# Differential attention: two maps taken one behind the other on VectorE, head squares on ScalarE

## The reference

```python
def probs(q, k):
    s = einsum(q, k) * scale + bias
    return softmax(where(visible, s, NEG_INF))

w = probs(q1, k1) - lam * probs(q2, k2)        # two maps of one head
out = einsum('bhqk,bkhd->bqhd', w, v)          # 4 heads of 128 columns
# per head: RMS norm over its 128 columns (diff_subln), scaled by 1 - lam_init
```

## Time and profile before

| | |
|---|---|
| median of three runs | 1819.9 us |
| profiled execution | 1820.2 us, its span 1818.9 us |
| TensorE busy | 1634.9 us (90%) |
| VectorE busy | 1139.2 us (63%) |
| ScalarE busy | 767.5 us (42%) |
| GpSimd busy | 53.1 us (3%) |
| read from memory | 217.31 MB |

### The profile page before, as it was taken

How to read it: one execution, slowest core, us unless ns; L and a number is a source line. 1 busy time by engine, 2 the same in 40 slices (tenths; PEclk the granted TensorE clock), 3 DMA queues, 4 the chain that set the end, 5 groups by cost and what they waited for, 6 DMA issues and landing times.

```text
span 1818.9 us, 24216 instructions
## 1 busy us (share of the span) xinstructions
PE 1634.9 (90%) x10180; PEld 1435.5 (79%) x10180; DVE 1139.2 (63%) x1898; ACT 767.5 (42%) x1260; POOL 53.1 (3%) x50
## 2 busy tenths in 40 slices
PE   7988997999989899979999998987799888999887
PEld 6978886999889888869998987766789767785455
DVE  5577556555546665465556668454977757777765
ACT  4545434444434454344444463422312234645334
POOL 0000011000000000100000001000000000000000
PEclk9999999999989899889999999966877799899998
DMA  8543334555545433245556532000002065331041
GB/s 268 164 140 124 109 105 162 178 189 186 186 136 170 132 122 114 95 139 185 185 186 192 183 110 77 1 1 1 1 1 94 0 209 156 114 129 45 23 156 70
DMA packets 151181, 219.94 MB, mean 121 GB/s; under 512 B 6230, under 2 KB 110686, under 8 KB 150432
## 3 DMA queue, kind: packets, MB, share of 16 engines
q1 hardware_dynamic: 151072, 218.39, 37.6%
HBM read 217.31 MB, written 1.06 MB: 120 GB/s over the span
## 4 chain that ended last, share of the span: by engine, by line
PE 72%; DVE 17%; ACT 7%; DMA 3%; issue 1%; SPq 0%; DVEq 0%
PE bank L381 17%; PE bank L383 16%; PE bank L382 16%; DVE weights_low L357 4%; PE bank L1901 4%; PE bank L846 2%; PE bank L1992 2%; PE bank L3227 2%; ACT weights_high L344 2%; PE bank L2187 2%; DVE place L2381 1%; PE bank L459 1%; PE bank L1958 1%; DMA place<-ple_w_dram 1%; PE bank L3188 1%
## 5 line engine op out<-in xcount | busy, mean ns | idle before, releaser
L357 DVE TENSOR_TENSOR weights_low<-place,weights_high 128x1024 fp32r<-128x1024 f32 (+2 forms) x387 | 450.1, 1206 | 189.4 <-ACT weights_high L344 188.9
L344 ACT ACTIVATE weights_high<-place 128x1024 fp32r<-128x1024 f32 (+2 forms) x387 | 378.7, 1031 | 140.7 <-DMA place<-w_down_dram 42.9
L381 PE MATMUL bank<-hT_high,weights_high 128*128 128x256 f32 x1152 | 336.7, 292 | 6.6 <-DVE hT_low L478 5.0
L383 PE MATMUL bank<-hT_high,weights_low 128*128 128x256 f32 x1152 | 329.2, 286 | 0.0
L382 PE MATMUL bank<-hT_low,weights_high 128*128 128x256 f32 x1152 | 328.7, 285 | 0.0
L381 PEld LDWEIGHTS bank<-hT_high,weights_high 128*128 128x128 f32 x1152 | 222.1, 193 | 12.7 <-DVE hT_low L478 5.8
L382 PEld LDWEIGHTS bank<-hT_low,weights_high 128*128 128x128 f32 x1152 | 221.9, 193 | 0.6
L383 PEld LDWEIGHTS bank<-hT_high,weights_low 128*128 128x128 f32 x1152 | 221.3, 192 | 0.0
L1901 PE MATMUL bank<-place,place 128*128 128x128 f32 x624 | 90.8, 312 | 26.2 <-DVE place L2348 10.4
L1901 PEld LDWEIGHTS bank<-place,place 128*128 128x128 f32 x624 | 87.0, 224 | 33.4 <-issue 22.6
L381 PE MATMUL bank<-weights_high,branchT_high 128*128 128x512 f32 x256 | 101.0, 395 | 0.0
(11 more groups left out here) (416 smaller groups left out, 3377.1 us busy)
## 6 DMA issues: line engine op xcount, KB each, us to landing
place<-w_in_dram SPq DMA_DIRECT2D x48, 1024.0 KB, 5.3
place<-w_up_dram SPq DMA_DIRECT2D x32, 1024.0 KB, 5.5
place<-w_down_dram SPq DMA_DIRECT2D x32, 1024.0 KB, 5.0
place<-even_w_in_dram SPq DMA_DIRECT2D x17, 1024.0 KB, 5.3
place<-w_out_dram SPq DMA_DIRECT2D x16, 1024.0 KB, 5.1
place<-odd_w_in_dram SPq DMA_DIRECT2D x16, 1024.0 KB, 5.3
place<-w_branch_dram SPq DMA_DIRECT2D x12, 1024.0 KB, 5.0
place<-ple_gate_dram SPq DMA_DIRECT2D x8, 1024.0 KB, 5.9
```

The lines of the kernel that those rows point to most:

```text
L344: nc.scalar.activation(high[:, lo:hi], self.raw[p % SLOTS][:, lo:hi], ACT.Copy).then_inc(*A("high", p, j))
L357: nc.vector.tensor_tensor(low[:, lo:hi], self.raw[p % SLOTS][:, lo:hi], high[:, lo:hi].bitcast(FP32), ALU.subtract).then_inc(*V())
L381: nc.tensor.matmul(out, left[0], right[0], start=first, stop=False)
L383: return nc.tensor.matmul(out, left[1], right[0], start=False, stop=last)
```

## The change

On VectorE the two maps of a differential head are taken one behind the other, both scores and maxima, and their reciprocals come later together, in a function of their own (`over_sums`). No filling stands between them: the steps are taken in bundles (`steps(count)`), for heads 1 to 3 between the second map's maxima and the reciprocals, and before the head's output is copied. On ScalarE the steps between the exponentials go away for the first eight maps but one bundle behind map 1; the rest of them come behind the copy of the turned probabilities. The counts are set so that from the fifth job on each engine is at the same step at the same place as before. The square and the sum of the heads leave VectorE; ScalarE squares each head with a sum (`squares`, two operations for the two token tiles), heads 0 to 2 behind the next copy of turned probabilities, head 3 behind its own output copy, just ahead of the square root. TensorE's order in attention is the same as before.

```diff
--- before.py
+++ after.py
@@ -1153,9 +1153,15 @@
         V.wait_ge(V)
         nc.vector.tensor_reduce(st[:, 0:1], s[:, 0:S], AX.X, ALU.max, negate=True).then_inc(*V())
         nc.vector.tensor_reduce(st[:, 1:2], s[:, S:], AX.X, ALU.max, negate=True).then_inc(*V("negmax", l, n))
+
+    def over_sums(n):
+        st = f.score_stats(n)
         V.wait_ge(("exp", l, n))
         nc.vector.reciprocal(st[:, 4:6], st[:, 2:4]).then_inc(*V("over_sums", l, n))
-        next(fill, None)
+
+    def steps(count):
+        for _ in range(count):
+            next(fill, None)
 
     def combined(h):
         (n1, n2) = maps_of(h)
@@ -1173,7 +1179,7 @@
         g, h = JOBS[job]
         n, width = maps_of(job)[0], (P, P, VDIM)[g]
         out, sums = f.heads_out[:, :, h * width:(h + 1) * width], f.score_stats(n)[:, 4:6]
-        next(fill, None)
+        steps(1 if job else 2)
         if h == 0 and g:
             V.wait_ge(("headsT", l, g - 1, 3))
         V.wait_ge(("out", l, job), V)
@@ -1185,19 +1191,15 @@
                 ins = nc.vector.tensor_scalar(out[:, t, :], b[:, at_:at_ + width], sums[:, r:r + 1], None, ALU.mult)
             ins.then_inc(*V())
         V.same("free", "out", l, job)
-        next(fill, None)
+        V.same("out_copied", l, job)
+        steps(1)
         if h == BRANCH_HEADS[g] - 1:
             finish_branch(g)
 
     def finish_branch(g):
         if g == 0:
-            sq = f.flat_junk[:, 0:TT * WB]
             ho = f.heads_out.rearrange("p t c -> p (t c)")
-            V.wait_ge(V)
-            nc.vector.tensor_tensor(sq, ho, ho, ALU.mult).then_inc(*V())
-            V.wait_ge(V)
-            nc.vector.tensor_reduce(stats[:, 48:56], split(sq, 8, P), AX.X, ALU.add).then_inc(*V())
-            k.rstd_vector(("subln", l), stats[:, 56:64], stats[:, 48:56], P, EPS_RMS, V)
+            k.rstd_vector(("subln", l), stats[:, 56:64], stats[:, 48:56], P, EPS_RMS, ("head_squares", l, DIFF_HEADS - 1))
             V.wait_ge(V)
             nc.vector.tensor_tensor(split(ho, 8, P), split(ho, 8, P), stats[:, 56:64].unsqueeze(2).to_broadcast([P, 8, P]),
                                     ALU.mult).then_inc(*V())
@@ -1219,8 +1221,14 @@
         for n in maps_of(job):
             scores(n)
         if g == 0:
+            steps((0, 3, 2, 2)[h])
+        for n in maps_of(job):
+            over_sums(n)
+        if g == 0:
             combined(h)
-        elif h == 1:
+        else:
+            steps(1)
+        if g and h == 1:
             heads_cut(g - 1)
         if job:
             weighted(job - 1)
@@ -1423,7 +1431,21 @@
         A.wait_ge(("negmax", l, n))
         nc.scalar.activation(s[:, 0:S], s[:, 0:S], ACT.Exp, bias=st[:, 0:1], accum_out=st[:, 2:3]).then_inc(*A())
         nc.scalar.activation(s[:, S:], s[:, S:], ACT.Exp, bias=st[:, 1:2], accum_out=st[:, 3:4]).then_inc(*A("exp", l, n))
-        next(fill, None)
+        if n == 1:
+            steps(2)
+        elif n >= 8:
+            steps(1)
+
+    def steps(count):
+        for _ in range(count):
+            next(fill, None)
+
+    def squares(h):
+        for t in range(TT):
+            n = 48 + DIFF_HEADS * t + h
+            A.wait_ge(("out_copied", l, h))
+            nc.scalar.activation(f.flat_junk[:, t * P:(t + 1) * P], f.heads_out[:, t, h * P:(h + 1) * P], ACT.Square,
+                                 accum_out=f.stats[:, n:n + 1]).then_inc(*A(*(("head_squares", l, h) if t else ())))
 
     def weighted(job):
         g, h = JOBS[job]
@@ -1431,9 +1453,11 @@
         if job >= 2:
             A.wait_ge(("out", l, job - 2))
         nc.scalar.activation(f.probsT[job % 2], k.bank("turned", l, job)[:, 0:SCORE_W], ACT.Copy).then_inc(*A("free", "turned", l, job))
-        next(fill, None)
-        next(fill, None)
+        if 0 < job < BRANCH_HEADS[0]:
+            squares(job - 1)
+        steps(4 if g == 0 and job < BRANCH_HEADS[0] - 1 else 2)
         if job == BRANCH_HEADS[0] - 1:
+            squares(job)
             k.rstd_scalar(("subln", l), f.stats[:, 56:64])
 
     def heads_cut(g):
```

## The result

| | before | after |
|---|---|---|
| median, same chip | 1817.83 us (1815.52 to 1820.47, 4 runs) | 1805.28 us (1804.27 to 1806.64, 4 runs) |
| profiled execution, its span | 1820.2, 1818.9 us | 1806.6, 1805.3 us |
| TensorE busy | 1634.9 us | 1630.0 us |
| VectorE busy | 1139.2 us | 1134.0 us |
| ScalarE busy | 767.5 us | 773.4 us |

The changed kernel takes 0.9931 of the time before (95% interval 0.9912 to 0.995), 12.55 us less. The forecast was 1806.5 us.

What follows compares the result with a forecast made beforehand. TensorE bounds the kernel, holding 72% of the chain. Attention wins 6.6 us in layer 0 and 8.3 in layer 1, 14.9 together, less 0.7 a layer for the clock: -13.5, forecast 1806.5 us, range 1801 to 1810 (72%).

Steps and rivals of the forecast that it cites:

- The first wait goes whole, and its slow clock with it.: TensorE before the first output product: wait of 4.39 us goes, with slow clock worth 1.7 us (layer 0), 5 (layer 1).
- Head 0 combined about 5.5 us after the first map.: VectorE in attention: head 0's combination ends about 5.5 us after the first map's start, where it took 9.44.
- VectorE stands 3.1 us for the high part of piece 57, harmless.: VectorE, cut of the fifth piece: waits 3.1 us for ScalarE's high part, where nothing else of it could run.
- "Its second and third output products wait 0.6 us each for ScalarE.": TensorE in attention: waits of 0.6 us each for ScalarE at the second and third output products.
- 2.4 us from the last head copies to the scaling, with the load exposed.: End of the heads: squares 0.62, exposed square-root table load 1.28, root and reciprocal make 2.4 us, where it was 3.23.
- "The squares therefore win only 3.2 - 2.4 = 0.8 us": Squares moved from VectorE to ScalarE: between last head copies and scaling they win only 0.8 us.
- the walk: Step-by-step timing of TensorE, VectorE and ScalarE through layer 0's attention in new order; scaling 46.8 us after first map's start.
- Scaling 47.5 us after the first map in both layers.: Scaling of the heads starts 47.5 us after the first map's start: 6.6 us won in layer 0, 8.3 in layer 1.
- 12.52 us from the scaling to the first branch product, moved as a whole.: Scaling to TensorE's first branch product: the stretch stays 12.52 us and starts that much earlier.
- 0.7 us a layer for the clock behind the heads.: Deduction for slow clock after TensorE's wait before the heads, 3.15 us instead of 2.44: a quarter of 2.75 us.
- The sum.: Whole kernel: 14.9 us won in both layers' attention, less 0.7 a layer for the clock, gives -13.5 us.
- The rival by which the gain is given back to the weights: Stages behind attention: the wait moves to the weights' stream from memory and the time is 1820; chance 8%.

Runs made afterwards that it cites:

- last head on VectorE: Changed kernel with the last head's two squares made by VectorE right behind its copies instead of by ScalarE; 1804.11 us, 0.9924 of before.
- order alone: Changed kernel with its new order on VectorE and ScalarE, but the heads' squares and sum left on VectorE as before; 1805.72 us, 0.9944 of before.
- squares alone: Kernel before, in its old order, with only the squares of the heads moved to ScalarE; 1816.61 us, 1.0011 of before.
- all squares on VectorE: Changed kernel with no squares on ScalarE, and the last head's copies, squares and scaling ahead of VectorE's last cut; 1791.49 us, 0.986 of before.
- the kernels with the scaling 4 and 5 us earlier still: Changed kernel with last head's copies, squares and scaling on VectorE ahead of its last cut, 0.9881 of before; the same with every square on VectorE, 0.986.
- the late copy: Changed kernel with ScalarE's high part of piece 60 back ahead of the copy of the first turned probabilities; 1809.86 us, 0.9963 of before.
- the first copy: Kernel before with only ScalarE's high part of piece 60 moved behind the copy of the first turned probabilities; 1814.75 us, 0.9999 of before.
- changed kernel again: The changed kernel, unaltered, profiled and timed a second time on another chip against the kernel before; 1802.33 us, 0.9922 of before.

## Why the prediction was right, point by point

- **The first wait goes whole, and its slow clock with it.** Right in both layers. The two kernels that split the order show the cause: without the earlier copy 0.64 us of the 4.39 come back, with the earlier copy alone 2.50 stay.
- **Head 0 combined about 5.5 us after the first map.** 5.60 us.
- **VectorE stands 3.1 us for the high part of piece 57, harmless.** 3.17 us at 135.90, and TensorE has no wait until 154.65.
- **"Its second and third output products wait 0.6 us each for ScalarE."** Wrong in number and size: the second and third wait for nothing, and the fourth waits 0.38 and 0.39 us.
- **2.4 us from the last head copies to the scaling, with the load exposed.** 2.52 us. The first pair of squares took 134.82 - 134.24 = 0.58 us, the last one, which is on the path, 159.86 - 159.15 = 0.71, where 0.62 were taken. The trace shows 0.02 us between the accumulator's read (159.66 + 0.18) and the load, and 0.02 between load and root. The experiment with the last head on VectorE, which takes the exposed load and the squares off the path, wins 1.26 us. The Trainium skill, page "ScalarE: Activation LUTs", section "What ACT_TABLE_LOAD costs", adds a drain of some 1380 ns to a switch. This trace does not agree: it has no gap of that size, and with such a drain on the path, by an estimate from that figure, about 2.6 us would have been won.
- **"The squares therefore win only 3.2 - 2.4 = 0.8 us".** This step failed. It priced the end of the stage alone. The order alone reaches the scaling 0.8 us earlier than order and squares together, and the squares alone leave the time where it was. The six early squares push the high parts behind them on ScalarE by 0.58 us a pair; the walk had two pairs inside VectorE's 3.1 us and TensorE's wait, did not name the third, and I did not set any of it against the 0.8. Against the order alone the last head copies end 1.5 us later: 0.6 is the third pair (the cut waits 2.22 us instead of 1.64), and 0.9 the first two, which the kernel with all squares on VectorE takes away (scaling 0.9 us earlier, the wait before the fourth output product gone). With the 1.26 us of the exposed load and last squares, both parts of the price are measured.
- **Scaling 47.5 us after the first map in both layers.** 48.3 and 48.9, so 5.8 and 6.9 us won instead of 6.6 and 8.3. 0.6 us in layer 1 are at its start: VectorE waits 1.02 us for map 1's scores (603.54) where it waits 0.42 in layer 0. The other 0.8 us are in both layers: 0.1 behind the last head copies (2.52 for 2.4), 0.7 before them, where the third pair of squares alone is 0.6. The slow operations beside GpSimd (below) are not in it: counted from TensorE's start of map 1's scores (113.99 and 602.58), the scaling comes after 47.64 us in both layers, though one of these operations of VectorE was slow in layer 0 only.
- **12.52 us from the scaling to the first branch product, moved as a whole.** 12.53 in both layers.
- **0.7 us a layer for the clock behind the heads.** The heads wait rose to 3.13 and 3.10 us (walk: 3.15), and the clock was 0.83 over ten microseconds in both layers [after: 163.00 and 651.00]. In layer 0 that is new (1.00 from 168 to 178 us before); layer 1 had 0.83 before too (658 to 668 us). It cost nothing up to the first branch product: the 12.53 us are the 12.52 of before, with shorter waits in them (in layer 0 0.91 us before the branch product instead of 1.26, and none instead of 0.99). The price that was deducted isn't there.
- **The sum.** 5.8 + 6.9 = 12.7 us at the scalings, and 12.55 us between the medians. The forecast had 14.9 - 1.4 = 13.5. It came out 1 us from the measured difference because its two errors (0.8 + 1.4 too much won in attention, 1.4 too much taken off) cancel in part; that is luck.

That the gain reached the end of the run unchanged is no more than an average, though. TensorE's windows from 258 to 267 us, before:

```profile
258.00:267.00 9.00, 5.52 (x42) 1.00 0.34 117
```

At the end of layer 0's attention both kernels wait the same 0.97, 0.58 and 0.66 us; before kept 1.00 there and the changed kernel got 0.62 [after: 258.00]. At 321 us the lead of 5.2 us was down to 0.15, and layer 1's first map starts at 601.32 against 601.29. In layer 1 the changed kernel is 6.9 us ahead at the scaling, 8.3 at the end of attention (764 us before) and 9.1 at the MLP's first squared activation; there the kernel before had the lower clock (0.81 from 760 to 770 us, the changed kernel 0.89 from 752 to 762). At the end of the span it is 13.6 us ahead. The stretch from the scaling to the first squared activation took 154.5 to 159.6 us in layer 0 over the ten profiles, and 158.9 to 161.9 in layer 1. The changed kernel's second profile, with the same attention and 1.4 us less behind it, shows that this part moves without any edit. What decides the clock there in one execution is left open.

The rival by which the gain is given back to the weights did not come true for the changed kernel: TensorE's waits for cut weights over the whole execution (releaser L357) are 16.5 us against 15.0 before, and the kernels with the scaling 4 and 5 us earlier still were faster again. But the runs do not exclude that a part is lost behind attention. In layer 0 the stretch behind the scaling took 154.5 to 157.6 us in the three profiles with the old order and 157.0 to 159.6 in the seven with the new one; in layer 1 the two groups overlap. And on the first chip the medians gained 4 to 5 us less than the scalings moved: the order alone 9.7 of 14.2 us, the late copy 5.6 of 10.8, the first copy 0.7 of 4.6. On the second chip this is not so (changed kernel again 16.4 us where the scalings moved 12.7, last head on VectorE 14.6 of 15.2). What makes the difference is open; a kernel of one group can't be compared with one of the other more closely than that.

## What to carry to other kernels

A wait of the bounding engine is traced back through two others: here ScalarE's copy was named, but VectorE's order of work held it for the larger part (no run moved the cut of 2.3 us between two maps alone), and moving what was named alone brought nothing in the end. When work is moved from one engine to another, charge it for every queue it passes on the new engine, and look what it pushes out from under a wait: a table load that was free there cost 1.3 us once squares stood ahead of it. A copy that is on the path should stand ahead of filling that isn't, on every engine; together with the last squares on VectorE that was worth about half as much again as the whole change here (0.9881 against 0.9922, with intervals that just overlap).

## What else the traces show of the hardware

Some VectorE operations took about twice their time beside an operation of GpSimd. In the changed kernel VectorE shows, in the 256-column form of L1173 and the 128-column form of L1175:

```profile
124.38 0.72 DVE L1173 TENSOR_SCALAR place<-place,place 128x256 f32<-128x256 f32 x1
...
147.70 0.80 DVE L1175 SCALAR_TENSOR_TENSOR place<-place,place,place 128x128 f32<-128x128 f32 x1
```

and GpSimd, at the same moments:

```profile
124.33 0.63 POOL L1526 TENSOR_SCALAR place<-place 128x512 f32<-128x512 f32 x1 [123.89 <-ACT place L1409]
...
137.38 1.36 POOL L1526 TENSOR_SCALAR place<-place 128x512 f32<-128x512 f32 x1 [8.43 <-ACT place L1409]
147.75 0.62 POOL L1526 TENSOR_SCALAR place<-place 128x512 f32<-128x512 f32 x1 [9.01 <-ACT place L1409]
```

The other rows of the two forms have 0.35. It goes both ways: beside the cut of 2.36 us at 135.90 the same operation of GpSimd took 1.36 instead of 0.62 us. In layer 1 the meeting at 612.92 stretches L1173 to 0.72 again, and the one at 636.33 leaves VectorE's 0.35 alone and takes 0.78 on GpSimd. The square at 154.74 in the kernel with all squares on VectorE, 0.57 instead of 0.29, has GpSimd's operation beside it too (154.52, 0.65 us). No run took GpSimd's work away, so that the two hold each other up is read from these rows and not tested.
